# Six of eight deferred modulation panels: summed by VectorE instead of multiplied by TensorE

## What is computed

```python
def modulation(cond, w_mod, b_mod):
    m = jax.nn.silu(cond) @ w_mod + b_mod
    m = m.reshape(-1, 1, 3 * D_MODEL)
    return jnp.split(m, 3, axis=-1)
...
        shift, scale, gate = modulation(c, w_mod[layer], b_mod[layer])
        shift_c, scale_c, gate_c = modulation(c_ctx, w_mod[layer], b_mod[layer])
        h = rms_norm(x, norm_w[layer]) * (1.0 + scale) + shift
        hc = rms_norm(xc, norm_w[layer]) * (1.0 + scale_c) + shift_c
...
        x = x + gate * y
        if not last:
            xc = xc + gate_c * y_c
```

## Time and profile before

| | us |
|---|---|
| median of 3 runs | 3623.99 (3620.34 to 3625.52) |
| profiled execution, device time | 3621.41 |
| profiled execution, span of the core | 3619.6 |
| busy in the span: TensorE / VectorE / ScalarE / GpSimd | 3411.6 / 1956.6 / 1846.3 / 434.0 |
| mean granted TensorE clock | 0.974 |
| deferred products, first to last start | 127.2 to 746.9 |

### The profile page before, as it was taken

How to read it: one execution, slowest core, us unless ns; L and a number is a source line. 1 busy time by engine, 2 the same in 40 slices (tenths; PEclk the granted TensorE clock), 3 DMA queues, 4 the chain that set the end, 5 groups by cost and what they waited for, 6 DMA issues and landing times.

```text
span 3619.6 us, 60203 instructions
## 1 busy us (share of the span) xinstructions
PE 3411.6 (94%) x25613; PEld 3065.3 (85%) x25613; DVE 1956.6 (54%) x2697; ACT 1846.3 (51%) x2906; POOL 434.0 (12%) x592
## 2 busy tenths in 40 slices
PE   6899999999899999999999999999989999899798
PEld 2577777778688999999999989999989899788797
DVE  1423222232455455666666465555576555899756
ACT  1344433322456744767766345555455564676444
POOL 0010101101000000000000010000010002688301
PEclk9999999999999999999999999999999999899899
DMA  9654555532233455555554545455545345333354
GB/s 384 220 174 141 170 178 190 200 124 98 76 123 128 157 175 176 169 192 178 171 188 157 182 158 175 169 169 168 170 147 169 123 136 180 114 127 129 106 180 146
DMA packets 157963, 589.83 MB, mean 163 GB/s; under 512 B 18352, under 2 KB 18384, under 8 KB 156032
## 3 DMA queue, kind: packets, MB, share of 16 engines
q1 hardware_dynamic: 135216, 497.64, 40.7%
q0 software_dynamic: 21904, 86.24, 7.0%
q10 hardware_dynamic: 576, 2.10, 0.2%
HBM read 583.69 MB, written 2.21 MB: 162 GB/s over the span
## 4 chain that ended last, share of the span: by engine, by line
PE 64%; PEld 12%; DVE 10%; DMA 6%; ACT 5%; issue 3%; PEldq 0%; POOL 0%; DVEq 0%; SPq 0%; ACTq 0%; POOLq 0%
PE psum_all L513 18%; PE psum_all L515 17%; PE psum_all L517 17%; PEld psum_all L517 4%; PEld psum_all L513 4%; PEld psum_all L515 4%; DMA raw<-in_stream 4%; DVE w_lo L459 2%; DMA mod_early<-in_stream 2%; PE psum_all L725 2%; ACT w_hi L452 1%; PE psum_all L1333 1%; DVE s_vd L2912 1%; PE psum_all L1303 1%; DVE s_vb L2911 1%
## 5 line engine op out<-in xcount | busy, mean ns | idle before, releaser
L513 PE MATMUL psum_all<-act_hi,w_hi 128*128 128x256 f32 (+1 forms) x6704 | 2055.6, 307 | 73.6 <-DVE act_lo L884 46.4
L515 PE MATMUL psum_all<-act_lo,w_hi 128*128 128x256 f32 (+1 forms) x6704 | 2019.0, 301 | 0.0
L517 PE MATMUL psum_all<-act_hi,w_lo 128*128 128x256 f32 (+1 forms) x6704 | 2017.6, 301 | 0.0
L459 DVE TENSOR_TENSOR w_lo<-raw,w_hi 128x1024 fp32r<-128x1024 f32 x866 | 1077.6, 1253 | 1248.0 <-ACT w_hi L452 1246.2
L513 PEld LDWEIGHTS psum_all<-act_hi,w_hi 128*128 128x128 f32 x6704 | 1293.9, 193 | 170.7 <-issue 101.7
L452 ACT ACTIVATE w_hi<-raw 128x1024 fp32r<-128x1024 f32 x866 | 910.5, 1057 | 854.7 <-DMA raw<-in_stream 852.6
L515 PEld LDWEIGHTS psum_all<-act_lo,w_hi 128*128 128x128 f32 x6704 | 1294.9, 193 | 42.5 <-issue 3.4
L517 PEld LDWEIGHTS psum_all<-act_hi,w_lo 128*128 128x128 f32 x6704 | 1293.5, 193 | 42.0
L699 POOL DMA_DIRECT2D mod_late<-in_stream x128 | 67.6, 532 | 660.5 <-PE psum_all L725 557.5
L961 POOL TENSOR_TENSOR ln_acc<-xT 128x256 f32<-128x256 f32 x8 | 5.9, 737 | 1018.2 <-DVE xT L1698 1018.2
L644 PE MATMUL psum_all<-mod_early,s_silu 128*32 128x512 f32 x256 | 57.6, 639 | 29.4 <-DMA mod_early<-in_stream 29.1
(11 more groups left out here) (475 smaller groups left out, 3316.6 us busy)
## 6 DMA issues: line engine op xcount, KB each, us to landing
raw<-in_stream SPq DMA_DIRECT2D x866, 512.0 KB, 3.3
mod_late<-in_stream POOLq DMA_DIRECT2D x128, 512.0 KB, 5.1
mod_early<-in_stream SPq DMA_DIRECT2D x64, 512.0 KB, 8.9
ssd_seg<-acs_rows POOLq DMA_DIRECT2D x8, 1536.0 KB, 6.7
ctxT<-in_ctx SPq DMA_DIRECT2D x2, 2048.0 KB, 13.9
xT<-in_x SPq DMA_DIRECT2D x1, 2048.0 KB, 15.9
fox_key_cum<-cum_rows POOLq DMA_DIRECT2D x1, 2048.0 KB, 8.7
out<-xT SPq DMA_DIRECT2D x4, 512.0 KB, 2.6
```

Source lines behind the costliest of these rows:

```text
L459: dve.tensor_tensor(w_lo[:, n % RING, :], raw[:, n % RING, :], w_hi[:, n % RING, :].bitcast(F32), ALU.subtract).then_inc(lo_ready, 1)
L513: pe.matmul(sums, w_hi[:, n % RING, cols], block.rhs(kk, True, block.width), start=(kk == 0), stop=False)
L515: pe.matmul(sums, w_hi[:, n % RING, cols], block.rhs(kk, False, block.width), start=False, stop=False)
L517: last = pe.matmul(sums, w_lo[:, n % RING, cols], block.rhs(kk, True, block.width), start=False, stop=(kk == block.kt - 1))
```

## The change

Panels 0 and 1 stay with TensorE. Panels 2 to 7 are summed by VectorE: for each unit (128 rows of `w_mod` on the partitions, 1024 columns) and each condition it adds the unit times the condition's value of that row, a scalar per partition, to a sum of 128 x 1024 (`late_add`). The first unit of a panel is a plain product, 15 follow as product-and-add in place. The sums of two panels and two conditions take 16 KB a partition, exactly the tile of the tokens, `xT`. The products over the partitions are left: TensorE multiplies each 128 x 128 part of a sum (as weights) with a column of ones, 16 products of one column for a panel, 8 for the last two panels (layer 1's gate), where the context's condition is left out. They come four slots after the panel's last unit. ScalarE's copy of the rows goes for these panels.

The deferred pairs are spread over 80 of the 88 slots rather than 84. `late_loads` waits for VectorE's sums where it waited for TensorE. The second load of the context leaves the sync queue; GpSimd's queue loads it behind the last sum and loads the tokens a second time behind the last turn, and the first output block waits for both.

```diff
--- before.py
+++ after.py
@@ -151,7 +151,10 @@
 
 EARLY_PAIRS = [(0, p, k) for p in range(4) for k in range(KT // 2)]
 LATE_PAIRS = [(0, p, k) for p in (4, 5) for k in range(KT // 2)] + [(1, p, k) for p in range(6) for k in range(KT // 2)]
-LATE_SLOTS = 84
+LATE_SLOTS = 80
+
+LATE_BY_PE = 2
+LATE_LAG = 4
 LAYER_ORDER = [(name, i) for name in "kv" for i in range(N_KV)] \
     + [(name, h) for h in range(N_Q) for name in ("q", "zb")] \
     + [(name, i) for i in range(SGU_GROUPS) for name in ("vg", "u")] + [("za", i) for i in range(SGU_GROUPS)]
@@ -257,8 +260,6 @@
                 u = first[section + name[-1]] + 2 * (block + i)
                 units.append([u, u + 1])
             out += [("split", u) for u in by_halves(units, LEAD[name])]
-            if name == "gate_in0":
-                out.append(("ctx", 0))
             continue
         if name in ("out0", "out1"):
 
@@ -605,6 +606,11 @@
             sp.dma_start(params[:, :], ins["params"]).then_inc(inputs_landed, 16)
             sp.dma_start(consts[:, :], ins["consts"]).then_inc(inputs_landed, 16)
 
+
+        late_sums = [[xT[:, 8 * s + 4 * v:8 * s + 4 * v + 4, :].rearrange("p k t -> p (k t)") for v in range(2)]
+                     for s in range(2)]
+        late_summed = sem("late_summed")
+
         def load_tokens(sp):
             sp.dma_start(xT[:, :, :], ins["x"]).then_inc(tokens_landed, 16)
             sp.dma_start(ctxT[:, :, :], ins["ctx"]).then_inc(tokens_landed, 16)
@@ -661,13 +667,13 @@
                                  small[:, 0:4], start=True, stop=True)
             last.then_inc(mod_turned, 1)
 
-        def mod_add(dve, layer, p, panel, bank=5):
+        def mod_add(dve, layer, p, panel, bank=5, conditions=2):
             dve.wait_ge(mod_turned, panel + 1)
             a = layer * 96 + p * 16
-            out = modulation[:, a:a + 16].rearrange("p (h b v) -> p b h v", h=2, v=2)
-            bias = param("b_mod", a, a + 16).rearrange("p (h b v) -> p b h v", h=2, v=2)
-            dve.tensor_tensor(out, psum[bank][:, 0:16].rearrange("p (b h v) -> p b h v", h=2, v=2), bias, ALU.add) \
-               .then_inc(mod_added, 1)
+            out = modulation[:, a:a + 16].rearrange("p (h b v) -> p b h v", h=2, v=2)[:, :, :, 0:conditions]
+            bias = param("b_mod", a, a + 16).rearrange("p (h b v) -> p b h v", h=2, v=2)[:, :, :, 0:conditions]
+            sums = psum[bank][:, 0:16].rearrange("p (b h v) -> p b h v", h=2, v=2)[:, :, :, 0:conditions]
+            dve.tensor_tensor(out, sums, bias, ALU.add).then_inc(mod_added, 1)
 
         def mod_scale(dve, layer, panels_added):
 
@@ -690,27 +696,84 @@
             for bank in (6, 7):
                 dve.memset(psum[bank], 0.0)
 
+        def late_conditions(p):
+
+            return 1 if LATE_PAIRS[p * PAIRS][0:2] in ((1, 4), (1, 5)) else 2
+
+        def late_sums_before(m):
+
+            return sum(late_conditions(i // KT) for i in range(LATE_BY_PE * KT, m))
+
+        def wait_late_used(eng, m):
+
+            if m // KT < LATE_BY_PE:
+                eng.wait_ge(mod_multiplied, len(EARLY_PAIRS) * 2 + m + 1)
+            else:
+                eng.wait_ge(late_summed, late_sums_before(m + 1))
+
         def late_loads(pool):
             pool.wait_ge(stage_done, 4 * late_stages)
             for m in range(2 * len(LATE_PAIRS)):
                 if m >= LATE_RING:
-                    pool.wait_ge(mod_multiplied, len(EARLY_PAIRS) * 2 + m - LATE_RING + 1)
+                    wait_late_used(pool, m - LATE_RING)
                 u = mod_units(*LATE_PAIRS[m // 2])[m % 2]
                 pool.dma_start(late_units[:, m % LATE_RING, :], ins["stream"][u]).then_inc(late_landed[m % LATE_RING], 16)
 
+            wait_late_used(pool, 2 * len(LATE_PAIRS) - 1)
+            pool.dma_start(ctxT[:, :, :], ins["ctx"]).then_inc(ctx_landed, 16)
+            pool.wait_ge(mod_turned, 12)
+            pool.dma_start(xT[:, :, :], ins["x"]).then_inc(ctx_landed, 16)
+
+        def late_turned(slot):
+
+            for lag, by_pe in ((1, True), (LATE_LAG, False)):
+                p = panel_ended(slot - lag)
+                if p is not None and (p < LATE_BY_PE) == by_pe:
+                    return p
+
         def late_tensor(pe, slot):
-            p = panel_ended(slot - 1)
-            if p is not None:
+            p = late_turned(slot)
+
+            if p is not None and p < LATE_BY_PE:
                 pe.wait_ge(mod_rows_ready, 4 + 2 * p + 2)
-
                 for b in range(4):
                     last = pe.matmul(psum[6 + p % 2][:, 4 * b:4 * b + 4],
                                      late_rows[b // 2][:, (b % 2) * P:(b % 2) * P + P], small[:, 0:4],
                                      start=True, stop=True)
                 last.then_inc(mod_turned, 1)
+            elif p is not None:
+                pe.wait_ge(late_summed, late_sums_before((p + 1) * KT))
+                if p >= 2:
+                    pe.wait_ge(mod_added, 4 + p - 1)
+                for v in range(late_conditions(p)):
+                    for h in range(2):
+                        for b in range(4):
+                            at = 4 * b + 2 * h + v
+                            last = pe.matmul(psum[6 + p % 2][:, at:at + 1],
+                                             late_sums[p % 2][v][:, (4 * h + b) * P:(4 * h + b + 1) * P],
+                                             const("ones", 0, 1), start=True, stop=True)
+                last.then_inc(mod_turned, 1)
             i = pair_after(slot)
-            if i is not None:
+            if i is not None and i // PAIRS < LATE_BY_PE:
                 late_multiply(pe, i)
+
+        def late_add(dve, i):
+
+            p = i // PAIRS
+            n = late_conditions(p)
+            for m in (2 * i, 2 * i + 1):
+                k, done = m % KT, late_sums_before(m)
+                dve.wait_ge(late_landed[m % LATE_RING], 16 * (m // LATE_RING + 1))
+                if k == 0 and p >= LATE_BY_PE + 2:
+                    dve.wait_ge(mod_turned, 4 + p - 1)
+                for v in range(n):
+                    sums, unit = late_sums[p % 2][v], late_units[:, m % LATE_RING, :]
+                    if k == 0:
+                        dve.tensor_scalar(sums, unit, s_late[:, k, v:v + 1], None, ALU.mult).then_inc(late_summed, 1)
+                    else:
+                        dve.wait_ge(late_summed, done - n + v + 1)
+                        dve.scalar_tensor_tensor(out=sums, in0=unit, scalar=s_late[:, k, v:v + 1], in1=sums,
+                                                 op0=ALU.mult, op1=ALU.add).then_inc(late_summed, 1)
 
         def late_multiply(pe, i):
             p, pair = i // PAIRS, i % PAIRS
@@ -738,10 +801,13 @@
                        .then_inc(mod_rows_ready, 1)
 
         def late_vector(dve, slot):
-            p = panel_ended(slot - 1)
+            i = pair_after(slot)
+            if i is not None and i // PAIRS >= LATE_BY_PE:
+                late_add(dve, i)
+            p = late_turned(slot)
             if p is not None:
                 layer, in_layer = LATE_PAIRS[p * PAIRS][0:2]
-                mod_add(dve, layer, in_layer, 4 + p, 6 + p % 2)
+                mod_add(dve, layer, in_layer, 4 + p, 6 + p % 2, late_conditions(p))
                 if (layer, in_layer) == (1, 5):
                     mod_scale(dve, 1, 4 + p + 1)
 
@@ -1652,7 +1718,7 @@
                 def take(dve, ps):
                     if b == 0 and not last:
                         dve.wait_ge(mod_added, 12)
-                        dve.wait_ge(ctx_landed, 16)
+                        dve.wait_ge(ctx_landed, 32)
                     for n, x in enumerate((xT, ctxT)[:parts]):
                         one = dve.scalar_tensor_tensor(out=x[:, b, :], in0=ps[:, n * T:(n + 1) * T],
                                                        scalar=mod_col(layer, b + 2 * KT, n), in1=x[:, b, :],
@@ -3057,11 +3123,6 @@
             stream = ins["stream"]
             n = {"split": 0, "early": 0}
             for kind, u in SEQUENCE:
-                if kind == "ctx":
-                    sp.wait_ge(mod_multiplied, 12 * KT)
-                    sp.wait_ge(mod_turned, 12)
-                    sp.dma_start(ctxT[:, :, :], ins["ctx"]).then_inc(ctx_landed, 16)
-                    continue
                 m = n[kind]
                 if kind == "split":
                     if m >= RING:
```

## The result

The changed kernel takes **3579.5 us** (median of 4 runs, 3577.0 to 3584.0), the kernel before 3624.7 beside it: a ratio of 0.9881, 95% interval 0.9866 to 0.9895. That is 45 us in the medians and 42.5 in the profiled spans (3619.6 and 3577.1). The forecast was 3574, 50 us less.

The account below looks back on a forecast made before the run. TensorE was taken to bound layer 0, with room on VectorE. 71.0 us removed less 21.3 added gave 49.7 off the profiled 3621.4: 3571.7, plus 2.6 for the median, 3574. Its own range was 3562 to 3586; with rivals A and B, 3561 to 3599.

Parts of the forecast that it names:

- What bounds: Layer 0, attention heads and gated chunks: TensorE is busy nearly throughout, so an instruction taken from its queue is time.
- Part 1: Deferred panels' products in layer 0: 48 of 64 pairs of units leave TensorE at 1.18 us each, 56.6 us less.
- Parts 2 and 3: TensorE's old turns: six go, 5.5 us; four waits for ScalarE's copy go, 5.5; half-clock stretch behind the second wait, 3.4.
- Part 4: New turns on TensorE: 80 one-column products at 0.25 us each add 20.0 us, of which 1.7 is covered.
- the other end: New turns on TensorE: the lower price of 0.23 us per one-column product, 18.2 us in all.
- The cover at block 21: End of block 21: one long turn falls into TensorE's existing 3.58 us wait for ScalarE's copy, hiding 1.7 us.
- Part 5: VectorE's sums: 160 operations at 1.19 us each, some 185 us beside TensorE; lateness charged at 3 us.
- Its lateness: Attention heads: VectorE's sums delay the softmax's links and stop TensorE, charged 3 us over ten blocks; ends 0 and 20.
- The walk through the slots: Attention heads, slot by slot: VectorE needs 28.3 of 29.7 us per two slots, nearly full, but lateness does not add up.
- Part 6: Moved DMAs and waits (units, context, tokens): cost 0; at worst one weight load 3 us later.
- rival B: The clock falls in the four long turns, 4 x 3.4 us, giving 3588; chance 0.09.
- one counterexample: At the first old wait, idleness, an old turn and one-column products followed one another at clock 1.00; held against rival B.

## Why the prediction held, and where it was off

- **What bounds** (TensorE's queue in layer 0): right. What was taken from it showed at the mark with its price.
- **Part 1**, 56.6 us for 48 pairs: nothing contradicts it. Going from two panels on TensorE to none shows the same price: 20.7 us of pairs and turns less 8 x 0.9 = 7.2 of long turns is 13.5; 10.0 was seen with 2.0 of waiting for the k heads and 1.7 of clock behind that wait.
- **Parts 2 and 3**, old waits and the half-clock stretch, 8.9 us with the four waits: right. Done alone they gave 10.6, of which 1.5 is the dip at block 21 that the prediction left in its sum.
- **Part 4**, the turns: taken at 0.25 us per product, measured 0.23, the other end that the text had named. 80 x 0.02 = 1.6 us too dear. The cover at block 21, 1.7 us: the wait shrank by 1.8.
- **Part 5**, VectorE: 1.19 us a step forecast, 1.22 measured (183.7 / 150). Its lateness was charged at 3 us; the waits of the trace show 0.4, and halving the work gives 1.0 at most. The walk through the slots was right that it does not add up.
- **Part 6**, moved loads: the gap is unchanged, the tokens' load shows 0.2 us at its place.
- **The step that failed** is a zero: that the clock stays up in the long turns. It was rival B, at 0.09. The four falls lost 12.8 us, close to the 4 x 3.4 of that rival, and the kernel before had lost 1.5 at block 21. Spreading the turns gave back 7.6 and halving them 7.7 beside their products. I had set it low for one counterexample (194.5 to 199.4 at 1.00). One row at full clock says little: two of 22 long turns went by at full clock too. The Trainium skill's rule (TensorE: Matmul & The Clock Gate, "What's actually happening") was the better guide here, and the trace of the changed kernel agrees with it four times out of four.

In sum, at the mark: 49.7 forecast, plus 2.6 of lateness not paid and 1.6 of cheaper turns makes 53.9; less the measured 44.0 leaves 9.9 missing. The clock took 12.8 - 1.5 = 11.3 that the forecast did not have, so 1.4 us are open. The forecast came within 6 us in part by luck: a zero that should have been 11 stood beside two terms set 4 us too dear. The chances were wrong in one place: B belonged near even, beside a forecast whose other terms it leaves alone.

## What to carry to other kernels

When the engine that bounds is full, price an instruction by the distance of its neighbours' starts, then look at what the replaced work leaves behind: here 80 one-column products cost 18 us by their starts and some 11 more by the clock. Put thin products into a dense stream in small portions. Here an in-order engine at 85%, with the new work last in its slot, held no one up; it became the bound when half as many sums again were added in the same place. Check the place of a copy against the slot in which its reader wants it: one number, 84 or 80, was worth 11 us in the kernel before and 3 in the changed one.

## What the runs showed of the hardware

- A long turn (16 products, each a 128x128 weight load with one column, 3.4 to 3.6 us at full clock) had a fall to 1.2 GHz within it or right behind it four times out of four in the changed kernel and 20 times out of 22 in five kernels. Turns of 8 products (1.8 us) and parts of four had none, except beside waits of about 4 us and more. With 32 columns per product there were four falls too, of 3.4 us each.
- The product-and-add of 1024 fp32 columns takes 1280 ns (1270 to 1287), and starts 1.22 us after the one before it when they queue; the plain product by a scalar takes 748.
- Eight one-column products with their own 128x128 weights take 1.81 us from the stream at full clock.
